# Stick-breaking attention: 1 - p ahead of p, the second head's product on GpSimd, the K and Q splits in eight pieces

## The reference, cut to what matters

```python
def sb_block(q, k, v, bias, q_pos, k_pos):
    z = jnp.einsum('bqhd,bkhd->bhqk', q, k) / math.sqrt(SB_HEAD_DIM)
    z = z + bias[None, :, None, None]
    mask = (k_pos[None, :] < q_pos[:, None])[None, None]
    log_1mb = jnp.where(mask, jax.nn.log_sigmoid(-z), 0.0)
    tail = lax.cumsum(log_1mb, axis=3, reverse=True) - log_1mb
    log_a = jnp.where(mask, jax.nn.log_sigmoid(z) + tail, -jnp.inf)
    a = jnp.exp(log_a)
    return jnp.einsum('bhqk,bkhd->bqhd', a, v)
```

## Time and profile before

| | before |
|---|---|
| median of three runs | 3438.86 us |
| lowest and highest | 3437.71 and 3443.4 us |
| the profiled execution, its own time | 3436.98 us |
| the profiled execution, its span | 3435.3 us |
| granted TensorE clock, mean share of full speed | 0.967 |

### The profile page before, as it was taken

The page is one execution under the profiler, slowest core; times in us unless marked ns, Lnnn a source line. Parts: engine busy times, 40 slices in busy tenths (PEclk is TensorE's granted clock), DMA queues, the critical chain, the costliest instruction groups (busy, mean ns, idle before and its releaser), DMA issues. The chain is left out here.

```text
span 3435.3 us, 59942 instructions
## 1 busy us (share of the span) xinstructions
PE 3168.9 (92%) x24506; PEld 2990.2 (87%) x24506; DVE 1779.4 (52%) x2670; ACT 741.2 (22%) x1267; POOL 988.2 (29%) x642
## 2 busy tenths in 40 slices
PE   6999999979999999998999878878999999999985
PEld 6888888869999999988899745556999999999985
DVE  4655656575444444465613188786154344434565
ACT  3111111121000000021301076666030000000121
POOL 5212222203232333334332313231233232323232
PEclk9999999989999999999999899899999999999997
DMA  3111111101111111111222555555111111111112
GB/s 102 44 45 45 42 47 39 45 26 44 49 43 49 43 49 43 49 54 57 75 93 93 191 180 191 171 196 187 44 44 43 49 43 49 43 49 43 57 54 75
DMA packets 72526, 247.52 MB, mean 72 GB/s; under 512 B 11058, under 2 KB 15154, under 8 KB 71986
## 3 DMA queue, kind: packets, MB, share of 16 engines
q1 hardware_dynamic: 64594, 221.15, 20.0%
q10 hardware_dynamic: 7776, 24.11, 1.9%
HBM read 218.88 MB, written 26.35 MB: 71 GB/s over the span
## 5 line engine op out<-in xcount | busy, mean ns | idle before, releaser
L1486 PE MATMUL psum<-xh,wh 128*128 128x352 f32 x4032 | 1327.6, 329 | 58.1 <-POOL wl L601 44.7
L1490 PE MATMUL psum<-xl,wh 128*128 128x352 f32 x4032 | 1303.6, 323 | 0.0
L1491 PE MATMUL psum<-xh,wl 128*128 128x352 f32 x4032 | 1302.7, 323 | 0.0
L599 POOL CAST wh<-raw 128x1024 fp32r<-128x1024 f32 x236 | 258.9, 1097 | 2028.2 <-PE psum L1486 1060.7
L1486 PEld LDWEIGHTS psum<-xh,wh 128*128 128x128 f32 x4032 | 766.0, 190 | 79.6 <-issue 56.2
L1490 PEld LDWEIGHTS psum<-xl,wh 128*128 128x128 f32 x4032 | 767.6, 190 | 2.1
L1491 PEld LDWEIGHTS psum<-xh,wl 128*128 128x128 f32 x4032 | 764.8, 190 | 0.0
L601 POOL TENSOR_TENSOR wl<-raw,wh 128x1024 fp32r<-128x1024 f32 x236 | 591.9, 2508 | 18.9
L1034 DVE TENSOR_TENSOR h<-h,psum 128x352 f32<-128x352 f32 x672 | 346.9, 520 | 341.6 <-PE psum L1491 341.4
L1486 PE MATMUL psum<-ah,wh 128*128 128x352 f32 x1344 | 446.4, 332 | 54.4 <-DVE h L1034 23.1
L1490 PE MATMUL psum<-al,wh 128*128 128x352 f32 x1344 | 440.7, 328 | 0.0
(11 more groups left out here) (181 smaller groups left out, 2764.7 us busy)
## 6 DMA issues: line engine op xcount, KB each, us to landing
raw<-in_wstream SPq DMA_DIRECT2D x236, 512.0 KB, 3.6
h<-in_kT_cache SPq DMA_DIRECT2D x64, 512.0 KB, 5.1
h<-in_v_cache SPq DMA_DIRECT2D x64, 512.0 KB, 4.8
h<-in_xT SPq DMA_DIRECT2D x3, 1408.0 KB, 10.8
out_kT_out<-work ACTq DMA_DIRECT2D x8, 528.0 KB, 2.7
out_vT_out<-work ACTq DMA_DIRECT2D x8, 528.0 KB, 2.7
qT_scratch<-work ACTq DMA_DIRECT2D x8, 528.0 KB, 2.7
h_scratch<-h SPq DMA_DIRECT2D x1, 4224.0 KB, 14.3
```

The lines of the kernel that those rows point to most:

```text
L599: nc.gpsimd.tensor_copy(wh[:, slot, :], raw[:, slot, :]).then_inc(split_hi, 1)
L1486: ins = mm(out, wh[:, slot, ws], mh, start=first, stop=False)
L1490: mm(out, wh[:, slot, ws], ml, start=False, stop=False)
L1491: return mm(out, wl[:, slot, ws], mh, start=False, stop=last)
```

## The change

Four edits, all in the attention stage:
1. ScalarE writes s (for the scan) first and p second, in each lane; a new semaphore `s_ready` counts s, `ps_done` still counts both.
2. Lane 0's product stays on VectorE; lane 1's product goes to GpSimd, 102 multiplications of up to 128 x 512. `a_done` becomes two semaphores, and all who waited for it wait for both.
3. The K and Q splits of the next pair no longer stand in a row: there are eight pieces of 128 x 512 (two casts and two subtractions of K, then of Q), one behind the product of each of the 1st to the 8th prompt step of the pair before. The outputs' splits stand one slot later than the copy that they need.
4. The transposes of the next pair's V rows go from the 7th to the 11th prompt step.

```diff
-    if slot < NATT and not ATT[slot].sample and ORDINAL[slot] % PER_PAIR == 6 and ATT[slot].pair + 1 < PAIRS:
+    if slot < NATT and not ATT[slot].sample and ORDINAL[slot] % PER_PAIR == 10 and ATT[slot].pair + 1 < PAIRS:
         events.append(("values", ATT[slot].pair + 1))
...
-            def split_rows(n, hi, lo):
-                slot = n // 2 % 2
-                item = 3 * (n // 2) + n % 2
-                pool.wait_ge(kqv_in[item % 2], 16 * (item // 2 + 1))
-                nc.gpsimd.tensor_copy(hi, raw[:, item % 2, :]).then_inc(k_hi_done, 1)
-                pool.wait_ge(k_hi_done, n + 1)
-                nc.gpsimd.tensor_tensor(lo, raw[:, item % 2, :], flat(hi), ALU.subtract).then_inc(kq_split, 1)
...
+            def split_part(j, part):
+
+                if part == 0 and j == 0:
                     pool.wait_ge(w_used, BEFORE)
-                elif j == 1:
+                elif part == 0 and j == 1:
                     pool.wait_ge(unit_done, U_Q)
+                elif part == 0:
+                    pool.wait_ge(z_done, LANES * PER_PAIR * (j - 1))
+                n = 2 * j + part // 4
+                item = 3 * j + part // 4
+                half = slice(part % 2 * CHUNK, (part % 2 + 1) * CHUNK)
+                hi, lo = ((wh, wl), (ah, al))[part // 4]
+                hi, lo, src = hi[:, j % 2, half], lo[:, j % 2, half], raw[:, item % 2, half]
+                if part % 4 < 2:
+                    pool.wait_ge(kqv_in[item % 2], 16 * (item // 2 + 1))
+                    nc.gpsimd.tensor_copy(hi, src).then_inc(k_hi_done, 1)
                 else:
-                    pool.wait_ge(z_done, LANES * PER_PAIR * (j - 1))
-                split_rows(2 * j, wh[:, j % 2, :], wl[:, j % 2, :])
-                split_rows(2 * j + 1, ah[:, j % 2, 0:TP], al[:, j % 2, 0:TP])
-
-            split_pair(0)
-            for j in range(PAIRS):
-                if j + 1 < PAIRS:
-                    split_pair(j + 1)
-                for out in range(PAIRS // 2 * j, PAIRS // 2 * (j + 1)):
...
+                    pool.wait_ge(k_hi_done, 2 * n + part % 2 + 1)
+                    last = nc.gpsimd.tensor_tensor(lo, src, flat(hi), ALU.subtract)
+                    if part % 4 == 3:
+                        last.then_inc(kq_split, 1)
+
+            for part in range(8):
+                split_part(0, part)
+            for slot in range(SLOTS):
+                if slot < NATT:
+                    i, s = slot, ATT[slot]
+                    pool.wait_ge(scan_done, LANES * (i + 1))
+                    pool.wait_ge(ps_done, LANES * (i + 1))
+                    a = weights[:, i % 3, 1, 0:s.width]
+                    nc.gpsimd.tensor_tensor(a, a, remain(i)[:, 1, CHUNK - s.width + 1:CHUNK + 1], ALU.mult)\
+                        .then_inc(a_done[1], 1)
+                    part = ORDINAL[i] % PER_PAIR if not s.sample else PER_PAIR
+                    if part < 8 and s.pair + 1 < PAIRS:
+                        split_part(s.pair + 1, part)
+                i = attended(slot - 1)
+                if i is not None:
+                    out = PAIRS // 2 * ATT[i].pair + ATT[i].query // 2
+                    at = (slice(None), ATT[i].pair, slice((ATT[i].query - 1) * P, (ATT[i].query + 1) * P))
                     pool.wait_ge(o_raw, out + 1)
...
-                    act.wait_ge(a_done, LANES * (i - 1))
+                    for e in range(LANES):
+                        act.wait_ge(a_done[e], i - 1)
...
-                    nc.scalar.activation(weights[:, i % 3, e, 0:s.width], z, ACT.Sigmoid, bias=plus)
                     nc.scalar.activation(remain(i)[:, e, CHUNK - s.width:CHUNK], z, ACT.Sigmoid, bias=minus, scale=-1.0)\
-                        .then_inc(ps_done, 1)
+                        .then_inc(s_ready, 1)
+                    nc.scalar.activation(weights[:, i % 3, e, 0:s.width], z, ACT.Sigmoid, bias=plus).then_inc(ps_done, 1)
...
                     if not s.first:
-                        dve.wait_ge(a_done, LANES * i)
+                        for e in range(LANES):
+                            dve.wait_ge(a_done[e], i)
...
-                    for e in range(LANES):
-                        dve.wait_ge(scan_done, LANES * i + e + 1)
-                        a = weights[:, i % 3, e, 0:s.width]
-                        nc.vector.tensor_tensor(a, a, r[:, e, lo + 1:CHUNK + 1], ALU.mult).then_inc(a_done, 1)
+                    dve.wait_ge(scan_done, LANES * i + 1)
+                    dve.wait_ge(ps_done, LANES * i + 1)
+                    a = weights[:, i % 3, 0, 0:s.width]
+                    nc.vector.tensor_tensor(a, a, r[:, 0, lo + 1:CHUNK + 1], ALU.mult).then_inc(a_done[0], 1)
```

More of the change, by code:

```diff
@@ L344, in yoco_step @@
         ps_done = sem("ps_done")
+        s_ready = sem("s_ready")
         scan_done = sem("scan_done")
         carry_done = sem("carry_done")
-        a_done = sem("a_done")
+        a_done = [sem("a_done0"), sem("a_done1")]
         turned = sem("turned")
@@ L652, in _ @@
             pool.sem_inc(consts, 1)
-            def split_rows(n, hi, lo):
-                slot = n // 2 % 2
-                item = 3 * (n // 2) + n % 2
-                pool.wait_ge(kqv_in[item % 2], 16 * (item // 2 + 1))
-                nc.gpsimd.tensor_copy(hi, raw[:, item % 2, :]).then_inc(k_hi_done, 1)
-                pool.wait_ge(k_hi_done, n + 1)
-                nc.gpsimd.tensor_tensor(lo, raw[:, item % 2, :], flat(hi), ALU.subtract).then_inc(kq_split, 1)
-            def split_pair(j):
-                if j == 0:
+            def split_part(j, part):
+                if part == 0 and j == 0:
@@ L664, in split_pair @@
                     pool.wait_ge(w_used, BEFORE)
-                elif j == 1:
+                elif part == 0 and j == 1:
                     pool.wait_ge(unit_done, U_Q)
-                else:
-                    pool.wait_ge(z_done, LANES * PER_PAIR * (j - 1))
-                split_rows(2 * j, wh[:, j % 2, :], wl[:, j % 2, :])
-                split_rows(2 * j + 1, ah[:, j % 2, 0:TP], al[:, j % 2, 0:TP])
-            split_pair(0)
-            for j in range(PAIRS):
-                if j + 1 < PAIRS:
-                    split_pair(j + 1)
-                for out in range(PAIRS // 2 * j, PAIRS // 2 * (j + 1)):
-                    part = out % (PAIRS // 2)
-                    at = (slice(None), j, slice(part * 2 * P, (part + 1) * 2 * P))
+                elif part == 0:
+                    pool.wait_ge(z_done, LANES * PER_PAIR * (j - 1))
@@ L1421, in _ @@
                     for e in range(LANES):
-                        dve.wait_ge(ps_done, LANES * i + e + 1)
+                        dve.wait_ge(s_ready, LANES * i + e + 1)
                         keep = r[:, e, lo:CHUNK][:, ::-1]
@@ L1425, in _ @@
                                                      ALU.mult, ALU.bypass).then_inc(scan_done, 1)
-                    for e in range(LANES):
-                        dve.wait_ge(scan_done, LANES * i + e + 1)
-                        a = weights[:, i % 3, e, 0:s.width]
-                        nc.vector.tensor_tensor(a, a, r[:, e, lo + 1:CHUNK + 1], ALU.mult).then_inc(a_done, 1)
+                    dve.wait_ge(scan_done, LANES * i + 1)
+                    dve.wait_ge(ps_done, LANES * i + 1)
+                    a = weights[:, i % 3, 0, 0:s.width]
+                    nc.vector.tensor_tensor(a, a, r[:, 0, lo + 1:CHUNK + 1], ALU.mult).then_inc(a_done[0], 1)
                     if s.sample and s.part:
+                        dve.wait_ge(scan_done, LANES * (i + 1))
                         nc.vector.tensor_copy(carry.rearrange("p (e o) -> p e o", o=1), r[:, :, lo:lo + 1])\
@@ L1777, in turned_over @@
                     for e in range(LANES):
-                        pe.wait_ge(a_done, LANES * n + e + 1)
+                        pe.wait_ge(a_done[e], n + 1)
                         rows = min(P, ATT[n].width)
```

## The result

The changed kernel takes 3466.6 us (median of four, 3460.36 to 3472.62), the kernel before 3438.28: ratio 1.0082, 95% interval 1.0068 to 1.0096. **It is 28 us slower; 3465 was forecast.** The size is right, and, as the experiments show, partly for the wrong reasons.

The account below looks back on a forecast made before the run. The attention stage was taken as bound by a loop of three engines, with VectorE and POOL hindering each other. Product and pieces +10 and the K wait +16 gave +26 us on 3437, so 3463, median 3465; range 3425 to 3500.

Parts of the forecast that it names:

- the loop of three engines: Attention stage: no engine is full; TensorE, VectorE and ScalarE wait for each other with one or two steps of slack.
- Part 5: POOL's queue: products stand behind the first piece's wait for K rows; 4 us a pair, +16 us for four pairs.
- the discount from 7.2 to 4 us a pair: K-row stall: about 2 us would be lost anyway to backlog, one or two free us behind it are used up.
- Parts 1 and 2 together: Second product to POOL, splits in eight pieces: shared time 4.8 us fuller, net +1.3 a pair, +10 us.
- The sum of shared time: Per pair, VectorE's busy time plus 0.85 of POOL's: 47.0 us before with 5.0 free, 51.8 after.
- The share of 0.85: Each us of POOL's work costs VectorE 0.85 us, taken from 0.95 in one place and 0.74 in another.
- Rival D: VectorE and POOL hold each other up fully, no free time won: 3509 us; with half won, 3490; chance 0.26.
- Part 3: ScalarE's s ahead of p: scans' waits end 0.59 us earlier; worth nothing by itself, pays for the product's detour.
- Part 4: V's transposes at the 11th step: VectorE's backlog covers them in four pairs; no own term, 0 to 3 us a pair.
- Rival B: Burst gone, pairs 1 to 6 each gain 8.6, pay 4.8 and 0.8; slack swallows stall: 18 us faster, 3421; chance 0.16.
- The signs named beforehand: POOL casts wait 8 to 11 us for K rows, POOL releases ScalarE, POOL product over 1.27 us, scans over 1367 ns.

Follow-up runs that it names:

- experiments 2: The kernel before, with only the K rows loaded early on SyncE: 3428.48 us, ratio 0.9966.
- Experiment 7: The changed kernel with the second head's product back on VectorE, K rows where they were: 3436.36 us, ratio 0.9998.
- 8: The changed kernel with the second head's product back on VectorE and the K rows loaded early: 3424.95 us, ratio 0.9961.
- experiment 4: The kernel before with the split in eight pieces, outputs' splits one slot later, both products on VectorE: 3414.63 us, ratio 0.9928.
- 9: The kernel before with s first, eight pieces and K rows early; products on VectorE, V's transposes at the 7th step: 3410.81 us, ratio 0.991.
- experiment 12: The kernel before with only V's transposes moved to the 11th step: 3446.72 us against 3435.19, ratio 1.0033.
- 10: The changed kernel with only V's transposes back at the 7th step: 3446.78 us, ratio to before 1.0018.

## Why the prediction was right, and where it was not

**What bounds the stage.** Right: the loop of three engines with a step or two of slack. VectorE lost 27 us of busy time and the stage grew.

**Part 5, the K wait.** Mechanism, place, the four pairs and the size of the hold-up were right: 7.2 us were read, and ScalarE's wait in pair 2 was 8.19. The step that failed is the discount from 7.2 to 4 us a pair, for backlog and later catching up. With the K rows early 36 us come back, 9 a pair, above even the upper end of 29. But the same edit is worth 11 us where no product stands behind the wait (experiments 2, and 7 against 8), so the wait itself costs 25 to 36 us, 6 to 9 a pair: at most 1 of the 7.2 us was made up. Why so little was is not shown.

**Parts 1 and 2 together, +10 us.** Two terms of opposite sign stood in one. Alone the pieces gain 25 us, and the move of the product to POOL costs some 6 (5.6 with V at the 11th step; the 1.9 with V at the 7th can't be told from nothing). The sum of shared time treated a us of POOL as equal wherever it stands. It is not: the same work gains 25 us when it is spread over eight steps (experiment 4), and ScalarE's waits for products, 27 us with the burst, fall to 5. The rows had said so (8.6 us between pairs 3 and 7), and I gave that gain to the rival. The sum also counted the outputs' splits twice, since they run in pair 7 too (POOL busy 5.85 us) and their hold-up is already in its 37.4 us; the free time was therefore put too low. The share of 0.85 is neither confirmed nor refuted by these times. POOL's product of 512 takes about 1.1 us beside an idle VectorE and at least 1.45 us in every other timeline row that holds one such product, and scans of 128 go from 579 to 1106 ns: the two engines hold each other up, and most of it lies where it costs nothing. The page "SBUF — State Buffer" of the Trainium skill, section "SBUF: two separate sides", calls this an exclusive lock for the whole instruction; these rows agree with it in kind, and do not decide between a share of 0.85 and one of 1. Rival D, full exclusion with no idle time won, falls by its second half: it wanted 54 us for products and pieces, while the move of the product costs about 6 and the pieces gain 25. POOL's product at 512 was estimated at 1.27 us; in the timeline above those of 512 and 256 take 1.78 together, beside an idle VectorE, and the second alone 0.73, so the first took nearer 1.1.

**Part 3, nothing by itself.** Alone it gains 10 us; not seen as a gain, since I followed the second product and not the first. Beside the pieces, it and the early K rows together add no more than the 4 us between experiments 4 and 9.

**Part 4, no term.** The reading was that VectorE's backlog at the 11th step hides V. It costs 11 us alone and 14 to 20 in the changed kernel (experiments 12; 8 against 9; 10). Failed: I compared VectorE's idle time at two steps and not TensorE's order within the slot. V's copy waits behind ScalarE's four activations, 256 columns wide at the 7th step and 512 at the 11th, and so TensorE waits 2.13 us for it and not 1.1 to 1.7. By itself that is 3 to 5 us over seven pairs. The clock was in no term at all: behind the longer wait it was mostly granted at the lower level, and TensorE was busy 10 to 15 us longer for the same matmuls. How the price divides between the two is open.

**The sum.** Experiment 7, all but the product on POOL, stands at 3436, 2 us below before. If V took 14 to 20 of that, the pieces and s first gave 16 to 22, less than the 35 that they give alone. The product on POOL with the wait for K rows ahead of it took the other 30. The forecast had +10 for the product and the pieces, +16 for the wait and 0 for the rest. It met the time by luck in its parts: an underrated wait, an unseen cost and an unseen gain cancelled. Rival B's mechanism, the burst, was real but overpriced: 8.6 less 0.8 us for each of six pairs is 47 us, and 25 were measured. Its price for the fuller share was too high as well (29 us against about 6), so that its sum of 18 lies near the 19 that the two measured terms give; what it had wrong is that the loop's slack would swallow the stall.

**The signs named beforehand.** ScalarE released by POOL came as described, and the K rows' wait too, if longer (12.3 to 12.8 us, not 8 to 11). POOL's product of 512 took 1.55 us, over 1.27, and POOL was busy 220 us where 204 were forecast. Scans of 512 did not grow (1330 against 1367 ns); those of 384 and 128 did (978 to 1466, 579 to 1106). Those of 384 also grow with the pieces alone, to 1199.

## What to carry to other kernels

Before work goes to an engine that already waits in program order for a transfer, list what will stand behind that wait: the product's move cost about 6 us by itself and 30 behind the K rows, and one transfer issued earlier gave it back. Splitting a burst on a helper engine, with no work removed, was the best part of this change (25 us), and it needed none of the others. Where a step makes TensorE wait longer, read its granted clock behind the wait as well: here V's move cost 11 to 20 us, and TensorE's busy time grew by 10 to 15 for the same matmuls. When a sum comes out right, time the parts alone all the same: the terms here were off by up to 30 us.

## What the runs showed of the hardware that was not expected

At the place of V's transposes the granted clock of the next 4 us was 0.50 to 0.69 behind 17 of 21 waits of 2.13 us, and 1.00 behind all 21 waits of 1.72 us or less (experiment 12).

POOL's multiplication of 512 columns into float32 takes less than its subtraction of 512 into the rounded type: two multiplications, of 512 and 256 columns, take 1.78 us together at 2083.47 in the changed kernel, 0.73 of it the one of 256, while the subtraction of 512 takes 1.27 alone. At 256 columns both take 0.73 us, and no run separates the operation from the type:

```profile
2088.60 1.27 POOL L673 TENSOR_TENSOR wl<-raw,wh 128x512 fp32r<-128x512 f32 x1
```
